# Seven block products instead of eight for all feed-forward tiles from the sixth on, with two weight sums made by adding DMA transfers

## The reference

```
g = h @ w_gate            # h: 512 x 1024 normed tokens, w_gate: 1024 x 2816
u = h @ w_up
x = x + (silu(g) * u) @ w_down          # w_down: 2816 x 1024; 0.5 * (...) in the second block
```

## Time and profile before

| | |
|---|---|
| median of 2 runs | 2688.94 us (2688.61 to 2689.26) |
| profiled execution, its own time | 2689.1 us |
| its span | 2687.3 us |
| mean granted TensorE clock | 0.996 |
| TensorE busy | 2642.6 us, 98% |
| VectorE busy | 1821.6 us, 68% |
| ScalarE busy | 1285.0 us, 48% |

### The profile page before, as it was taken

How to read it: one execution, slowest core, us unless ns; L and a number is a source line. 1 busy time by engine, 2 the same in 40 slices (tenths; PEclk the granted TensorE clock), 3 DMA queues, 4 the chain that set the end, 5 groups by cost and what they waited for, 6 DMA issues and landing times.

```text
span 2687.3 us, 37446 instructions
## 1 busy us (share of the span) xinstructions
PE 2642.6 (98%) x15123; PEld 2235.7 (83%) x15123; DVE 1821.6 (68%) x2738; ACT 1285.0 (48%) x1956; POOL 26.7 (1%) x45
## 2 busy tenths in 40 slices
PE   9989999999999999999999999999999999999998
PEld 8777888988777888987889888888777888888996
DVE  7885746656885746666657556899978844674664
ACT  6784423336784423344323334445688453442332
POOL 0000000000000000000000000000000000000000
PEclk9999999999999999999999999999999999999999
DMA  6303233334203223232232242222222422223322
GB/s 217 94 2 110 95 90 107 94 90 163 79 2 110 102 86 110 95 106 82 83 114 95 90 158 79 72 78 71 78 92 90 133 95 94 94 92 91 116 84 74
DMA packets 80429, 255.80 MB, mean 95 GB/s; under 512 B 9600, under 2 KB 12800, under 8 KB 79872
## 3 DMA queue, kind: packets, MB, share of 16 engines
q1 hardware_dynamic: 77744, 240.29, 27.7%
q0 software_dynamic: 2512, 13.11, 1.4%
HBM read 241.30 MB, written 8.39 MB: 93 GB/s over the span
## 4 chain that ended last, share of the span: by engine, by line
PE 89%; DVE 6%; ACT 4%; issue 1%; DMA 0%; DVEq 0%; SPq 0%; ACTq 0%
PE PS L1607 22%; PE PS L1608 22%; PE PS L1609 22%; PE PS L1636 4%; PE PS L1638 4%; PE PS L1637 4%; PE PS L1886 1%; DVE WLO L2419 1%; PE PS L1868 1%; ACT WHI L1974 1%; PE PS L1566 1%; PE PS L1655 1%; PE PS L1654 1%; PE PS L1656 1%; PE PS L1832 0%
## 5 line engine op out<-in xcount | busy, mean ns | idle before, releaser
L2419 DVE TENSOR_TENSOR WLO<-WR,WHI 128x1024 fp32r<-128x1024 f32 (+4 forms) x482 | 518.6, 1080 | 402.8 <-ACT WHI L1974 400.4
L1974 ACT CAST WHI<-WR 128x1024 fp32r<-128x1024 f32 (+4 forms) x482 | 448.4, 931 | 525.4 <-PE PS L1609 410.9
L1607 PE MATMUL PS<-HHI,WHI 128*128 128x512 f32 x1680 | 670.4, 399 | 0.9 <-ACT Z L2086 0.9
L1609 PE MATMUL PS<-HHI,WLO 128*128 128x512 f32 x1680 | 654.9, 390 | 0.0
L1608 PE MATMUL PS<-HLO,WHI 128*128 128x512 f32 x1680 | 654.9, 390 | 0.0
L1607 PEld LDWEIGHTS PS<-HHI,WHI 128*128 128x128 f32 x1680 | 315.9, 188 | 70.6 <-issue 5.0
L1609 PEld LDWEIGHTS PS<-HHI,WLO 128*128 128x128 f32 x1680 | 315.5, 188 | 66.9
L1608 PEld LDWEIGHTS PS<-HLO,WHI 128*128 128x128 f32 x1680 | 316.0, 188 | 66.1 <-issue 4.4
L1607 PE MATMUL PS<-FHI,WHI 128*128 128x512 f32 x693 | 269.6, 389 | 0.0
L1608 PE MATMUL PS<-FLO,WHI 128*128 128x512 f32 x693 | 269.6, 389 | 0.0
L1609 PE MATMUL PS<-FHI,WLO 128*128 128x512 f32 x693 | 269.6, 389 | 0.0
(11 more groups left out here) (434 smaller groups left out, 4426.3 us busy)
## 6 DMA issues: line engine op xcount, KB each, us to landing
WR<-in_stream SPq DMA_DIRECT2D x338, 512.0 KB, 3.3
WR<-in_stream SPq DMA_DIRECT2D x64, 384.0 KB, 3.0
WR<-in_stream SPq DMA_DIRECT2D x64, 320.0 KB, 2.9
xkeep<-X POOLq DMA_DIRECT2D x3, 2048.0 KB, 9.1
X<-xkeep POOLq DMA_DIRECT2D x24, 256.0 KB, 5.6
WR<-in_stream SPq DMA_DIRECT2D x16, 328.0 KB, 4.3
ROT<-RQ SPq DMA_DIRECT2D x40, 64.0 KB, 2.0
X<-in_xin SPq DMA_DIRECT2D x8, 256.0 KB, 5.7
```

What stands on the lines that cost most here:

```text
L1607: e.matmul(out, hi[:, i, :], xhi, start=first, stop=False)
L1609: t = e.matmul(out, lo[:, i, :], xhi, start=False, stop=final)
L1974: e.copy(hi, raw).then_inc(S["act_high"], 1)
L2419: e.tensor_tensor(lo, raw, hi.bitcast(F32), ALU.subtract).then_inc(S["dve_low"], 1)
```

## The change

Three of four stages make tiles 5 to 21 by seven products, the third (f = 2) tiles 8 to 21: 65 tiles where there were 36. So that tiles by seven can follow each other:
- The sums are held twice over: TS, THI and TLO have two buffers of three sums (TS and TLO share their place). Two of the four weight sums are made by transfers. `tget` (SP) loads half of the up weights a second time into TS, `tadd` 0 (POOL) adds half of the gate weights to it by a DMA with an accumulating write. `tadd` 1 (POOL) adds the other half of the up weights onto the first half of the up slot in WR, in place, so the slot's split serves as the fourth sum. `tsum` keeps two adds; `thi` and `tlo` are one step each, 1536 wide; the up slot is split whole.
- u1 and u2 change places. The second `snap` stays in PSUM. `gs` and `cc` are one step of 512 columns each.
- `eight` and `seven` no longer add `silu`, `mul`, `fhi`, `flo` at once but as chains that come when their inputs are due; times in the planner's table are changed for the feed-forward steps, and the planner holds `load` and `high` of a slot until the transfers are due (ADDING, LOADING).
- Some semaphores are merged to make room; nothing else waits on them.

```diff
-SEVEN = range(5, FT, 2)
-PRODUCTS = ((0, 0, True), (1, 0, True), (2, 0, True), (0, 1, False), ...)
+SEVEN = {f: tuple(range(5 if f != 2 else 8, FT)) for f in range(4)}
+PRODUCTS = ((0, 0, True), (2, 0, True), (1, 0, True), (0, 1, False), ...)
+ADDING, LOADING = 8.0, 4.0
+def two_before(f, j):
+    i = SEVEN[f].index(j)
+    return SEVEN[f][i - 2] if i >= 2 else None
+TIMES.update(gs=(("dve", 0.62),), silu=(("act", 0.55),), mul=(("dve", 0.65),), fhi=(("act", 0.54),), ...)
...
     def load(self):
-        if self.next_load < len(self.slots):
+        self.due += 1
+        self.load_due()
+    def load_due(self):
+        while self.due and self.next_load < len(self.slots):
+            before = self.pair_of.get(self.next_load - RAW)
+            if before and not self.summed(before):
+                return
             self.add("load", self.next_load)
+            if self.next_load in self.summed_up:
+                self.spawn(self.up_sum(self.pair_of[self.next_load]))
             self.next_load += 1
+            self.due -= 1
...
+    def activated(self, f, j):
+        scaled = self.add("gs", f, j)
+        self.free(("gate", f, j), ("dve_gs", scaled))
+        yield scaled
+        self.add("silu", f, j)
+    def multiplied(self, f, j):
+        yield from self.added(("silu", f, j), *((("flo", f, j - 2),) if j >= 2 else ()))
+        yield from self.until(("silu", f, j))
+        done = self.add("mul", f, j)
+        ...
+        yield done
+        yield self.add("fhi", f, j)
+        self.add("flo", f, j)
+    def gate_joined(self, f, j, keys):          # ww, gs, silu after u5
+    def up_joined(self, f, j, key):             # cc, then multiplied, after u6
...
     def seven(self, f, gate, up, i, up0, j):
-        self.run(lambda: ("tlo", f, j, 1) in self.n)
         for u in range(7):
+            if u == 1:
+                self.run(lambda: ("tlo", f, j) in self.n)
...
-            if u == 0 or u == 2:
-                self.add("snap", f, j, u // 2)
-            elif u == 1:
+            if u == 0 or u == 1:
+                self.add("snap", f, j, u)
+            elif u == 2:
+                self.run(lambda: ("flo", f, j - 2) in self.n)
                 self.add("pd", f, j)
...
+    def up_sum(self, pair):
+        yield LOADING
+        self.add("tadd", *pair, 1)
+        yield ADDING - LOADING
+        self.ready.add(pair)
+        self.advance()
     def weight_sums(self, f, j):
         yield from self.added(("sslo", f, 3))
         last = max(k for k, pair in self.pair_of.items() if pair == (f, j))
+        used = two_before(f, j)
+        if used is not None:
+            yield from self.added(("srow", f, used, 1, 3))
+            yield from self.until(("srow", f, used, 1, 3))
+        self.add("tget", f, j)
+        yield self.add("tadd", f, j, 0)
+        yield ADDING
         while last - RAW not in self.low:
             yield 0.1
-        yield self.add("tsum", f, j)
+        if used is not None:
+            yield from self.added(("srow", f, used, 3, 3))
+            yield from self.until(("srow", f, used, 3, 3))
+        done = self.add("tsum", f, j)
+        self.load_due()
         self.advance()
-        if j - 2 in SEVEN:
-            yield from self.until(("srow", f, j - 2, 5, 3))
-        for k in range(2):
-            self.add("thi", f, j, k)
-        for k in range(2):
-            yield ("thi", f, j, k)
-            self.add("tlo", f, j, k)
+        yield done
+        yield self.add("thi", f, j)
+        self.add("tlo", f, j)
...
-    THI = sb("THI", 192, [4, T], F32R)
-    TLO = sb("TLO", 206, [4, T], F32R)
-    WT = sb("WT", 200, [2, T]), sb("WT2", 214, [2, T])
+    THI = sb("THI", 192, [2, 3, T], F32R)
+    TLO = sb("TLO", 206, [2, 3, T], F32R)
+    TS = sb("TS", 206, [2, 3, T])
...
             elif kind == "tsum":                                   # DVE
-                settle(e.tensor_tensor(WT[0][:, 0, :], gate[:, 0:T], up[:, 0:T], ALU.add))
-                e.tensor_tensor(WT[1][:, 0, :], up[:, 0:T], up[:, T:2 * T], ALU.add)
-                settle(e.tensor_tensor(WT[0][:, 1, :], WT[0][:, 0, :], up[:, T:2 * T], ALU.add))
-                e.tensor_tensor(WT[1][:, 1, :], WT[0][:, 1, :], gate[:, T:2 * T], ALU.add)...
+                added(q, f, j, 0)
+                settle(e.tensor_tensor(t2, t1, up[:, T:2 * T], ALU.add))
+                e.tensor_tensor(t4, t2, gate[:, T:2 * T], ALU.add).then_inc(S["dve_scale"], 1)
...
+            elif kind == "tadd":                                   # POOL
+                f, j, i = a
+                k_gate, k_up = o.slot_of["seven", f, j]
+                if i:
+                    q.wait_ge(s_w[k_up % RAW], 16 * (k_up // RAW + 1))
+                    if PAIR_COUNT[f, j]:
+                        q.wait_ge(s_sum[1], 16 * PAIR_COUNT[f, j])
+                else:
+                    q.wait_ge(s_get, 16 * PAIR_COUNT[f, j] + 16)
+                block = weights_from(k_up)[:, T:2 * T] if i else weights_from(k_gate)[:, 0:T]
+                e.dma_start(block_sum(f, j, i), block, accum_op=ALU.add).then_inc(s_sum[i], 16)
...
+            elif kind == "tget":                                   # SP
+                f, j = a
+                if two_before(f, j) is None:
+                    q.wait_ge(S["dve_xlow"], n["sslo", f, 3])
+                else:
+                    q.wait_ge(S["pe_prod"], o.product_end[f, two_before(f, j), 1])
+                if PAIR_COUNT[f, j]:
+                    q.wait_ge(s_sum[0], 16 * PAIR_COUNT[f, j])
+                e.dma_start(block_sum(f, j, 0), weights_from(o.slot_of["seven", f, j][1])[:, 0:T]).then_inc(s_get, 16)
```

More of the change, by code:

```diff
@@ L217 @@
                 ((1, 2), (1, 3), (2, 1), (3, 1)), ((2, 2), (3, 2), (2, 3), (3, 3)))
+PAIR_COUNT = {p: i for i, p in enumerate((f, j) for f in SEVEN for j in SEVEN[f])}
+def two_before(f, j):
+    i = SEVEN[f].index(j)
+    return SEVEN[f][i - 2] if i >= 2 else None
+FFN_WEIGHTS = ("w_gate", "w_up", "w_down", "ffn1_w_in_2", "ffn1_w_out_2", "ffn2_w_in_2", "ffn2_w_out_2")
+TIMES.update(gs=(("dve", 0.62),), silu=(("act", 0.55),), mul=(("dve", 0.65),), fhi=(("act", 0.54),), flo=(("dve", 0.61),),
+             tsum=(("dve", 1.4),), tlo=(("dve", 1.68),), pd=(("dve", 0.4),), ww=(("dve", 0.92),), cc=(("dve", 0.7),),
+             snap=(("act", 0.36),), srow=(("pe", 0.3625),), padd=(("dve", 1.35),))
 class Order:
@@ L242, in __init__ @@
         self.first, self.pair_of, self.product_end, self.products = {}, {}, {}, 0
+        self.summed_up, self.ready = set(), set()
+        self.due = 0
         self.tokens = 0
@@ L255, in add @@
             self.engine_end["act"] += 1.28
-        for engine, us in TIMES.get(step[0], ()):
+        for engine, us in self.times(step):
             t = self.engine_end[engine] = max(t, self.engine_end[engine]) + us
@@ L262, in add, with times @@
         return step
+    def times(self, step):
+        if step[0] in ("low", "high") and self.slots[step[1]][0] in FFN_WEIGHTS:
+            size = self.slots[step[1]][3] * self.slots[step[1]][5]
+            return (("dve", 0.06 + 0.00107 * size),) if step[0] == "low" else (("act", 0.09 + 0.00086 * size),)
+        return TIMES.get(step[0], ())
     def take(self, key, ring="main"):
@@ L284, in advance @@
             k = self.next_split
+            if k in self.summed_up and self.pair_of[k] not in self.ready:
+                break
             if k - RAW in self.pair_of and not self.summed(self.pair_of[k - RAW]):
@@ L524, in ffn @@
         m = NORM_FFN[f]
-        for pair in SEVEN:
+        for pair in SEVEN[f]:
             at_ = self.slots.index((gate, i, 0, DT, pair * P, P))
             self.pair_of[at_] = self.pair_of[at_ + 1] = (f, pair)
+            self.summed_up.add(at_ + 1)
         self.x["sv", f] = list(self.x_now)
@@ L1458, in combination, with weights_from, added, block_sum @@
         return SUMS[k][:, :, :].rearrange("p r t -> p (r t)")
+    def weights_from(k):
+        size = o.slots[k][3] * o.slots[k][5]
+        return stream[offset[k]:offset[k] + P * size].rearrange("(p n) -> p n", p=P)
+    def added(q, f, j, i):
+        q.wait_ge(s_sum[i], 16 * PAIR_COUNT[f, j] + 16)
+    def block_sum(f, j, i):
+        return WR[:, o.slot_of["seven", f, j][1] % RAW, 0:T] if i else TS[:, SEVEN[f].index(j) % 2, 0, :]
+    def first(f, j):
+        return P1[SEVEN[f].index(j) % 2][:, :]
+    def sums(f, j):
+        b = SEVEN[f].index(j) % 2
+        return (x[:, b, :, :].rearrange("p u c -> p (u c)") for x in (TS, THI, TLO))
     def block_weights(f, j, u):
@@ L1468, in block_weights @@
             return hi[:, 4:8, :], lo[:, 4:8, :]
-        i = {1: 1, 2: 0, 3: 3, 5: 2}[u]
-        return (x[:, i, :].rearrange("p (r c) -> p r c", r=4) for x in (THI, TLO))
+        if u == 5:
+            hi, lo = weights(k_up)
+            return hi[:, 0:4, :], lo[:, 0:4, :]
+        i = {1: 0, 2: 1, 3: 2}[u]
+        return (x[:, SEVEN[f].index(j) % 2, i, :].rearrange("p (r c) -> p r c", r=4) for x in (THI, TLO))
```

(21 more changed lines are left out.)

150 lines of the change are left out of this document (80 added, 70 removed).

## The result

The changed kernel takes 2738.96 us (two runs, 2738.36 and 2739.56), the one before 2688.94; ratio 1.0187, 95% interval 1.0171 to 1.0204. That is 78 us above the forecast and outside its range; it went the other way, though within the 2% that I had given 0.90. The profiled execution took 2738.36 us, span 2736.6.

A forecast was written before the change was run, and what follows sets the result against it. TensorE's matmuls were taken to bound the kernel. From the profiled 2689.1 us: minus 24.4 of matmul work, minus 11.4 of third-stage waits, plus 4 and 3.6 for new waits, gave 2660.9, predicted as 2661; range 2653 to 2700.

The forecast's parts named there:

- What the adding transfers must meet: Tiles by seven: `tget` then `tadd` take 7.2 us after TensorE's release, inside 12.1 us, so TensorE need not wait.
- 84 matmuls at 0.120 against 48 at 0.227, 24.4 us for 29 tiles: Feed-forward stages: each tile made by seven products instead of eight saves TensorE 0.84 us, 24.4 us over 29 tiles.
- The third stage, 11.4 us: Third feed-forward stage: TensorE's waits at its first sevens, with half-clock tails, vanish with a later first seven; 11.4 us won.
- VectorE 8.85 us, 88%, no bound: Tiles by seven: VectorE's steps sum to 8.85 us in 10.07, leaving 1.22 us to spare.
- The prices of the transfers: Sums' transfers: `tget` near a 320 KB row of 2.9 us, `tadd` 4.3, together 7.2, bounds 5.9 and 12.0.
- Allowance 12.1: Tiles by seven: the two transfers may take 12.1 us from TensorE's release before `pd` comes late.
- First sevens, 4 us, and one late `pd`, 3.6: Waits costing 2 us twice at the starts of sevens in the stages, plus one late `pd` behind a VectorE burst, 3.6 us.
- An add by DMA at half the rate: Adding transfers: two source reads might halve a copy's speed; `tadd` at most 8.6 us, both transfers 11.5, still under 12.1.
- VectorE's: Rival: in tiles by seven VectorE's waits make it the bound, 11.75 us per tile, 2770 us; chance 0.17.
- late in every tile: Rival: `tget` and `tadd` together exceed 12.1 us; at 13.1 each of 65 tiles waits 1 us, 2726; chance 0.07.
- The third, waits kept in the third stage or at the first sevens: Rival: third stage's waits move to tile 8, or all stages' first sevens wait 3.5 us more; 2672 us; chance 0.12.
- No waits at all: Whole kernel: TensorE never waits, 2653.3 us, the low end of the forecast's own range.

The follow-up runs named there:

- three adds: Against the changed kernel: `tget` and `tadd` 0 dropped, VectorE makes the weight sums in three steps instead of two; 2654.91 us, ratio 0.9872.
- with odd tiles from tile 5 on: Changed kernel, its SP order kept, with tiles by seven only at 5, 7, ... 21 in all four stages; 2676.52 us, ratio 0.9955.
- with `tget` first: Changed kernel with each `tget` issued on SP's queue ahead of the two loads that stood before it; 2661.39 us, ratio 0.9896.
- the two plain copies above, issued by POOL: Copies from the changed kernel with `tget` moved from SP's queue to POOL's, in front of its `tadd`; 2677.56 us, ratio 0.9959.
- the version with four steps: Three VectorE adds replacing `tget` and `tadd` 0, as in the 2654.91 us version, with one add done twice; 2659.60 us, ratio 0.9892.
- the wait moved and the order kept: Changed kernel with the wait on `s_sum[0]` moved from `tget` to `tadd` 0 on POOL, SP's order kept; 2748.91 us, ratio 1.0227.

## Why the prediction was wrong

The step that failed is in "What the adding transfers must meet": "`tget` on SP's queue may go when TensorE has done u1 of tile j-2". That was the wait written at `tget`. Its real release is what stands ahead of it in its queue: two loads that wait for `tsum` of the tile before. I had worked out where `tsum` falls and where the loads go, and did not put `tget` behind them; the planner puts steps in a list by its times, and the list has the loads first. With this release the transfers are no chain of 7.2 us with 12.1 allowed, but part of a ring of 12.05 us against a tile of 10.07. The sign that I had named for this case was there: tiles 12 us apart, TensorE waiting for `pd`, and VectorE idle before `tsum` waiting for a DMA, 1.95 to 3.39 us. Moving the one step gave 2661.39 for a forecast of 2661.

Point by point:
- *84 matmuls at 0.120 against 48 at 0.227, 24.4 us for 29 tiles.* Right: 24.6 us by the starts in the traces of the kernel before and of three adds.
- *The third stage, 11.4 us.* Right in size (11.1 by the starts in the trace), wrong in its reason: with odd tiles from tile 5 on it went as well, so the later first tile was not needed.
- *VectorE 8.85 us, 88%, no bound.* Right. In the changed kernel it was at 0.72 for want of input; with 9.5 us of steps per tile TensorE waited nowhere in a tile by seven, with 10.3 it began to.
- *The prices of the transfers.* `tget` 2.9: measured 3.3 with nothing ahead, 4.7 behind the loads, whose company I had priced at nothing. `tadd` 4.3: measured 4.2, and 5.1 with `tget` first. Their sum, 7.2, was 8.4 to 9.7. The nearest row was not the one of 320 KB: the trace of before also has 256 KB on SP's queue in 2.2 us (out<-X) and, eight in a row, in 5.7 (X<-in_xin).
- *Allowance 12.1.* About right for one chain; but the wait on `s_sum[0]` makes a second bound of 10.07 on the two transfers, which the sum did not have. It does not bind in the changed kernel.
- *First sevens, 4 us, and one late `pd`, 3.6.* With `tget` first the tiles by seven lose 6.1 us (661.3 for 655.2), where the two terms have 7.6: about right in size, but not in place. No stage has a wait at its first tile by seven. `tlo` is late by 0.59 and by 0.11 us at tiles 20 and 21 of each stage, and `pd` by 0.2 us twice. I had reason for waits elsewhere, so that the sum came out at 2661 is in part luck. The other 2 of the 8 us above the time with no wait lie outside the tiles by seven. With three adds the 6.1 are gone and 1.6 remain above that time.
- *DMA share 0.55.* Measured 0.56 in the changed kernel, whose tiles are 12 us apart, and 0.65 with `tget` first: too low for the pace that it was meant for.
- *An add by DMA at half the rate.* At 256 KB no run here shows it: the adding transfers have medians of 4.2 and 5.4 us in the changed kernel, 5.1 and 4.1 with `tget` first, the two plain copies above, issued by POOL, 3.2 and 3.9; that is 1.1 to 1.7 times, with the collisions of each in it. The rule of half the rate (the Trainium skill, Collectives: The Full Stack, "The bandwidth ceiling: the fold count and why AG ≠ RS ≠ AR", given there for ReduceScatter against AllGather) would make it twice. These traces do not show that, and it was not what made the kernel slower.

The rivals: VectorE's was refuted. The second, "late in every tile", had the right picture, `tsum` held by its transfers at 65 tiles and 2726, at a chance of 0.07 and with the wrong cause: I looked for length and not for what lets them start. The third, waits kept in the third stage or at the first sevens, did not come: in the changed kernel and with `tget` first no stage waits at its first tile by seven. "No waits at all", 2653.3, was reached within 2 us by three adds.

## What to carry to other kernels

A step's release is the latest of its own waits and of everything ahead of it on its queue. For each step added to an in-order queue, write down what the entry just ahead of it waits for, and follow that back; if it comes back to the step itself one tile later, sum the turn and hold it against the tile. Such a ring showed no cost at every other tile (36 tiles, 2676.52 us) and cost 78 us when the tiles followed each other, most of it in the long runs, so a recipe that is free where it was tried says little about a denser use.

## What was not expected of the hardware

Waits of TensorE of 0.2 to 0.6 us left the granted clock at 2.4 GHz (1.00 after the 0.53 us wait at 508.51 of the version with four steps), one of 2.85 us was followed by 0.50, and one of 3.38 us by 1.00. Six of 39 waits for `pd` were followed by half clock in the changed kernel, 14 of 39 with the wait moved and the order kept, and those 14 are what made it slower still. The same transfer of 256 KB took 3.3 us ahead of 1 MB of loads and 4.7 behind them.
